# Residual updates of a streaming encoder step: the product with the reciprocal norm formed on GpSimd

## What is computed

```python
def rms_norm(x, g):
    y = x * lax.rsqrt(jnp.mean(x * x, axis=-1, keepdims=True) + EPS)
    return y * g

x = x + rms_norm(mixed,             P['g_post_mix'][l])
x = x + rms_norm(memory_attend(...), P['g_post_mem'][l])
x = x + rms_norm(h @ P['w_down'][l], P['g_post_ff'][l])
```

## Time and profile before

| | us |
|---|---|
| median of 3 runs | 2842.84 |
| the three runs | 2836.05, 2842.84, 2852.88 |
| span of the profiled execution | 2829.8 |
| PE busy | 2645.4 (93%) |
| DVE busy | 1442.4 (51%) |
| ACT busy | 800.5 (28%) |
| POOL busy | 826.6 (29%), 331 low parts |

### The profile page before, as it was taken

The page is one execution under the profiler, slowest core; times in us unless marked ns, Lnnn a source line. Parts: engine busy times, 40 slices in busy tenths (PEclk is TensorE's granted clock), DMA queues, the critical chain, the costliest instruction groups (busy, mean ns, idle before and its releaser), DMA issues.

```text
span 2829.8 us, 47053 instructions
## 1 busy us (share of the span) xinstructions
PE 2645.4 (93%) x18040; PEld 2417.1 (85%) x18040; DVE 1442.4 (51%) x2236; ACT 800.5 (28%) x1460; POOL 826.6 (29%) x335
## 2 busy tenths in 40 slices
PE   8999999999989899999889999999999898999996
PEld 7679888877988799999777798888779787999995
DVE  4661364354464754245656614633554647453366
ACT  4342112234324311111223421122343243111112
POOL 3113222311333143344321132232113232344342
PEclk9999998999999999999999999989999999999998
DMA  4102112222222122222221121122222231222222
GB/s 142 38 23 86 60 47 77 76 75 70 83 71 90 41 83 83 84 83 84 68 77 31 31 90 56 47 84 72 73 71 81 64 94 53 83 84 88 82 83 85
DMA packets 65655, 204.87 MB, mean 72 GB/s; under 512 B 7920, under 2 KB 15984, under 8 KB 65328
## 3 DMA queue, kind: packets, MB, share of 16 engines
q10 hardware_dynamic: 47808, 174.08, 20.2%
q1 hardware_dynamic: 17648, 28.04, 3.0%
HBM read 191.07 MB, written 11.03 MB: 71 GB/s over the span
## 4 chain that ended last, share of the span: by engine, by line
PE 82%; DVE 9%; DVEq 5%; issue 2%; ACT 1%; DMA 0%; SPq 0%; ACTq 0%
PE job L356 65%; PE outp L410 4%; PE scores L385 4%; DVE rstd L1012 3%; PE turn L399 2%; PE job L365 2%; DVEq L1039 2%; PE scores L286 1%; PE scores L388 1%; DVE arena L1003 1%; DVEq L1075 1%; DVE rstd L1020 1%; DVEq L991 1%; DVE x L1040 1%; DVEq L1018 0%
## 5 line engine op out<-in xcount | busy, mean ns | idle before, releaser
L356 PE MATMUL job<-arena,w_hi 128*128 128x288 f32 (+1 forms) x9984 | 1774.2, 299 | 29.9 <-DVE arena L977 8.5
L356 PEld LDWEIGHTS job<-arena,w_hi 128*128 128x128 f32 x9984 | 1491.0, 191 | 52.5 <-issue 20.7
L629 POOL TENSOR_TENSOR w_lo<-raw,w_hi 128x1024 fp32r<-128x1024 f32 x331 | 826.4, 2497 | 1972.3 <-ACT w_hi L648 1972.3
L356 PE MATMUL job<-arena,w_lo 128*128 128x288 f32 (+2 forms) x4992 | 1085.5, 297 | 0.0
L356 PEld LDWEIGHTS job<-arena,w_lo 128*128 128x128 f32 (+1 forms) x4992 | 815.3, 190 | 0.0
L648 ACT ACTIVATE w_hi<-raw 128x1024 fp32r<-128x1024 f32 x331 | 349.7, 1057 | 1086.5 <-PE job L356 899.7
L986 DVE TENSOR_TENSOR tmp<-job,rstd 128x576 f32<-128x576 f32 x70 | 53.0, 758 | 328.1 <-PE job L356 323.6
L410 PEld LDWEIGHTS outp<-probT,v 128*64 128x64 f32 (+2 forms) x992 | 107.5, 145 | 95.7 <-ACT probT L741 46.2
L410 PE MATMUL outp<-probT,v 128*64 128x128 f32 (+2 forms) x992 | 155.4, 284 | 27.5 <-DVE arena L1083 18.4
L286 PE MATMUL scores<-q,const 128*128 128x288 f32 (+1 forms) x296 | 100.0, 476 | 68.2 <-ACT q L709 58.7
L385 PE MATMUL scores<-k,q 128*128 128x256 f32 (+10 forms) x400 | 151.0, 461 | 12.7 <-DVE k L1379 4.4
(11 more groups left out here) (150 smaller groups left out, 1794.1 us busy)
## 6 DMA issues: line engine op xcount, KB each, us to landing
raw<-in_w ACTq DMA_DIRECT2D x332, 512.0 KB, 3.6
bias<-in_bias SPq DMA_DIRECT2D x16, 256.0 KB, 3.4
x<-in_x SPq DMA_DIRECT2D x4, 576.0 KB, 9.1
cs<-in_rope SPq DMA_DIRECT2D x4, 576.0 KB, 4.5
out_o_bandk<-k SPq DMA_DIRECT2D x8, 288.0 KB, 4.3
out_o_bandv<-tmp SPq DMA_DIRECT2D x8, 288.0 KB, 4.6
out_y<-x SPq DMA_DIRECT2D x1, 2304.0 KB, 6.9
bias<-in_mem SPq DMA_DIRECT2D x8, 256.0 KB, 3.6
```

The costliest lines, as they stand in the source:

```text
L356: mm = pe.matmul(ps[0:m, po:po + nn], w[:, s, c:c + m], x[:, k, so:so + nn], start=(k == 0 and w is WHI and x is hl[0]), stop=(k == kt - 1 ...
L629: nc.gpsimd.tensor_tensor(WLO[:, u % RING, :], RAWS[:, u % RAW, :], WHI[:, u % RING, :].bitcast(F32), ALU.subtract).then_inc(lo_done, 1)
```

## The change

In `update_x` DVE no longer forms the scaled sum. After the reciprocal it raises `inverse`. POOL waits for that and forms `UPD[k % 2]` = M[k] x rstd for each of the eight tiles, raising `normed`; from the third tile on it waits until DVE has used the buffer (`act_asked`, two tiles back). DVE waits for `normed` and does X[k] = UPD x gain + X[k] in one instruction, without a drain. To place the products in POOL's order, its loop now runs over layers, with the 164 units of one written out, and the products of an update stand behind the low part of unit `placed + LEAD - 2`, two units past the last one that ACT has placed by then. 24 products per layer, 48 in all.

```diff
+U_MIXED = U_MLA_IN + MLA_HEADS + 3 * U_BRANCH + U_RET + U_BAND + KT
+UPDATES = U_MIXED + 2, U_MIXED + U_MEM + KT // 2, UNITS
...
-            with pool.Fori(0, DEPTH * UNITS, RING) as g:
-                for j in range(RING):
-                    lo(g + j, j)
-            for j in range(LEAD - 1):
-                lo(DEPTH * UNITS + j, j)
+            for u in range(LEAD - 1):
+                lo(u, u)
+            with pool.Fori(0, DEPTH) as l:
+
+                def scale_update(site):
+
+                    pool.wait_ge(inverse, l * len(UPDATES) + site + 1)
+                    for k in range(KT):
+                        if k >= 2:
+
+                            pool.wait_ge(act_asked, l * REQS + AHEAD["ask"] + RET_ASKS + site * KT + k - 1)
+                        nc.gpsimd.tensor_tensor(UPD[:, k % 2], M[:, k], rstd[:, :], ALU.mult).then_inc(normed, 1)
+
+                for u in range(LEAD - 1, UNITS + LEAD - 1):
+                    lo(l * UNITS + u, u)
+                    for site, placed in enumerate(UPDATES):
+                        if u == placed + LEAD - 2:
+                            scale_update(site)
...
-                    def normed(k):
-                        v.scalar_tensor_tensor(out=UPD[:, k % 2], in0=M[:, k], scalar=g_col(name, k),
-                                               in1=rstd[:, :], op0=ALU.mult, op1=ALU.mult)
-
...
                     invert(rstd[:, :])
-                    normed(0)
+                    dve.sem_inc(inverse, 1)
                     for k in range(KT):
-                        dve.drain()
-                        ask(v.tensor_tensor(X[:, k], X[:, k], UPD[:, k % 2], ALU.add))
-                        if k + 1 < KT:
-                            normed(k + 1)
+                        n["normed"] += 1
+                        dve.wait_ge(normed, l * len(UPDATES) * KT + n["normed"])
+                        ask(v.scalar_tensor_tensor(out=X[:, k], in0=UPD[:, k % 2], scalar=g_col(name, k), in1=X[:, k],
+                                                   op0=ALU.mult, op1=ALU.add))
                         if k:
                             low(k - 1)
                     low(KT - 1)
```

More of the change, by code:

```diff
@@ L137 @@
 GATES = 3 * KT + RET_HEADS
-REQS = 3 * KT + RET_HEADS + RET_HEADS // 2
+RET_ASKS = RET_HEADS + RET_HEADS // 2
+REQS = 3 * KT + RET_ASKS
 READY = 42
@@ L266, in build @@
         phase_done = sem("phase_done")
+        inverse, normed = sem("inverse"), sem("normed")
         settled = [sem(f"settled_{e}") for e in ("pe", "dve")]
@@ L948, in _ @@
             with dve.Fori(0, DEPTH) as l:
-                n = counts("job", "gate", "ready", "ask", "done", "item", "store", "rounded")
+                n = counts("job", "gate", "ready", "ask", "done", "item", "store", "rounded", "normed")
                 at = dict(job=0)
@@ L1543, in counted @@
     want = dict(job=JOBS, unit=UNITS, gate=GATES, ready=READY, ask=REQS, item=ITEMS, done=ROOTS,
-                store=STORES, sq=SQUARES, rounded=ROUNDS)
+                store=STORES, sq=SQUARES, rounded=ROUNDS, normed=3 * KT)
     assert all(want[k] + AHEAD.get(k, 0) == v for k, v in n.items()), n
```

## The result

The changed kernel takes 2863.06 us (median of 4 runs, 2860.58 to 2869.91) against 2844.77 us (4 runs, 2836.05 to 2852.88): ratio 1.0074, 95% interval 1.0048 to 1.0099. In a second comparison on one chip it was 2863.23 against 2847.79 us, ratio 1.0060 (1.0041 to 1.0079). It is slower by 15 to 18 us.

What follows compares the result with a forecast made beforehand. DVE was taken to set the pace in the updates, 2.31 us a tile. First and second updates +15.6, third +10.4, together +26.0: 2829.8 + 26.0 + 13.0 = 2868.8, say 2869 us; range 2852 to 2888.

Steps and rivals of the forecast that it cites:

- Direction and cause: In the updates, GpSimd's products and DVE's two-input instructions take turns, so their times add up: 0.9% slower.
- part 2: GpSimd's 128x576 product in the updates: 1.35 us, with a saving possible down to about 1.25.
- part 3: Reciprocal's end to last addition: 8 products, 8 additions, 6 low parts in turns, 21.0 us against 17.16; +3.9 per update.
- Tail: Rounding, square, four matmuls and root behind an update's last addition: claimed unchanged.
- Third update: Weight's low part stands ahead of the first product; last addition +4.7 us, update +5.2, twice: +10.4.
- half charge for slow squares: Third update: paired additions make the second wait about 0.9 us for PE at 1.2 GHz; half taken.
- The base of the sum: Whole kernel: the median lies 13.0 us above the profiled span of 2829.8, taken as what surrounds a span.
- Waits and queues, loop: Engine queues at the updates and GpSimd's written-out loop: nobody waits for the low parts behind; the loop costs nothing.
- Without exclusion: Rival: engines don't exclude each other; pace 1.77 us, -3.1 us four times, third updates about nothing; 2830 us, chance 0.06.
- rival of cheap products and hidden turns: Updates: products of 0.86 to 1.15 us, or DVE start-up partly hidden under turns; within 0.5%, say 2850; chance 0.13.
- The clock rival: PE stays at 1.2 GHz to the end of first and second updates: 2879 us, or 2890 if longer; chance 0.15.
- The signs named beforehand: Updates: DVE instructions of 1.9 to 3.4 us, none inside a product; period near 2.7; reciprocals about 4 further apart; POOL +65.

Runs made afterwards that it cites:

- no_read: Changed kernel, but GpSimd fills each product buffer with a constant instead of M x rstd, a 128x1 product ahead of each fill: 2841.91 us (one run).
- before_again: Unchanged copy of the kernel before, profiled once more: span 2846.1 us, six updates together 153.29 us.
- after_again: Unchanged copy of the changed kernel, profiled once more: span 2856.2 us, six updates together 170.09 us.
- four_buffers: Changed kernel with four product buffers instead of two, so GpSimd may run four tiles ahead: 2863.42 us (10 runs), ratio 1.0066.

## Why the prediction held, point by point

**Direction and cause.** Right. The rows of before already had one addition at 2.74 us and one low part of GpSimd at 3.65, and the same two-way standing still fills the changed update. Products nobody waits for cost 1.16 us each, more buffers gave nothing, half the products cost half of the loss, and a fill that doesn't read cost DVE nothing. The Trainium skill, "SBUF — State Buffer", section "Who interferes with whom", says that a VectorE instruction with two SBUF inputs contends with a GpSimd instruction that reads SBUF, not with one that only writes; the first half agrees with the 1.97 us additions, the second with the 0.81 us ones beside fills in no_read.

**Price of a product (part 2).** Taken as 1.35 alone: 1.38 measured (2.75 for two). The estimate of 1.40 by the Trainium skill, "GPSIMD Engine Reference", section "Elementwise — side-by-side cycle accounting", was as near, on the other side. In its turn it counts 1.28 only: GpSimd's instruction is issued (849.32) before DVE's ends (849.97), and part of its start seems to be over by then; the prediction named this saving (1.25) and didn't take it.

**Sum to the last addition (part 3).** 21.0 us forecast, 19.94 measured. This is the term that was mis-sized: a turn is 1.28 + 0.61 + 0.73 = 2.62 us (2.63 from row to row) instead of 1.35 + 1.44 = 2.79. On both engines an instruction that waits ends sooner behind the other than it would take alone (1.28 for 1.38, 0.61 for 0.73), and DVE's 0.62 behind GpSimd stood in rows 6. Per tile the change takes away 0.67 for the scaled sum and 0.18 of drain, 0.85 in all, and puts in 1.28 + 0.61 - 0.73 = 1.16. The difference of 0.31 over seven tiles is 2.2 us. The first addition starts 1.55 us behind the reciprocal's end instead of 0.99, behind a product instead of a scaled sum, which makes the 2.78 of 19.94 - 17.16; 0.11 of the tail brings it to the 2.89 measured (forecast: 3.9).

**Tail.** Called unchanged. Right in the first update, where the root came 3.04 us behind the last addition before (858.36 - 855.32) and 3.15 after (864.37 - 861.22), the 0.11 above.

**Third update.** 5.2 forecast, 2.6 to 3.6 measured over the pairs of runs. The last addition came 3.67 us later against 4.7 forecast, for the same reason as above. The half charge for slow squares had the wrong sign. It rested on additions that come in pairs 1.4 us apart; but with two buffers GpSimd starts a product only behind the addition two tiles back, the additions ended 2.6 us apart, and only the last two came as a pair (1430.06 and 1431.52). The tail from the last addition to the reciprocal was 4.53 and 3.48 us in the two layers of before, 4.13 and 4.53 in before_again, but 3.49 and 3.48 in after, 3.47 and 3.79 in after_again: in three of the four third updates of before the last squares fell into a spell at the lower level, in the changed kernel the spell was over, or nearly, by then. What ends it isn't shown.

**The sum.** It is 4 x 2.9 + 2.6 + 3.6 = 17.8 us in place of 26.0, so the difference was forecast 8.2 us too large. The forecast time of 2869 still lay only 6 us above the median of 2863.06. That is luck in part: the median of before rose from 2842.84 to 2844.77 with a fourth run, and both medians scatter by a few us.

**The base of the sum.** The 13.0 us between the span of the first profile and the median were taken for what surrounds a span. Wrong: the profiled run of the changed kernel took 2860.58 us with a span of 2858.7, so 1.9 surround it. The rest is about what the short MLP of that one execution (399.5 us, where 409 to 411 is usual) is worth. It didn't hurt, because the difference was set on the median.

**Waits and queues, loop.** As said: GpSimd's next low part came 7.00 us after its last product, and the written-out loop cost nothing.

**The rivals.** Without exclusion the first and second updates would have gained 0.9 us (no_read), not 3.1. The rival's pace of 1.77 took no account of PE's first tiles at 1.2 GHz (3.53 and 2.63 us there), which leave it behind for good. And the third updates, where it put about nothing, came about 5 us shorter in no_read; all six together were 138.7 us against 153, so 14 us less where it named 12, by other parts. (A fill of 0.57 us is shorter than a product, so this is a bound rather than the price of the exclusion.) Of the rival of cheap products and hidden turns the second half came true in part: a turn was 0.16 us shorter than forecast, but the products weren't cheap. The clock rival didn't come about: PE's pause ahead of the update grew from 7.72 to 9.45 us, and it was still back at the 2.4 GHz level by the second tile of the first update (squares of 1.13 us at 849.67) and by the third tile of the other three first and second updates, and stayed there. In the third updates the level did fall again midway (squares of 1.24 us at 1423.68, of 2.15 at 1426.28), in the thin work that the rival named, but it was back for the last squares. The signs named beforehand were seen: additions of 1.9 to 2.0 us, none of them done inside a product, a pace of 2.63. The two reciprocals of a first or second update are 2.9 further apart where "about 4" stood, and POOL's busy time grew by 85, where 65 stood, because an instruction that stands still counts as busy.

## To carry to other kernels

Before work is handed from DVE to GpSimd, ask what both read. If the product and what DVE runs meanwhile each take two tensors from SBUF, the two times add up: here GpSimd's 1.16 us in its turn replaced 0.85 us of DVE. The trace of before answers it, without an experiment, in the longest instances of two-input instructions (2.74 us where the median is 0.76) and what runs beside them. And look at the next bound: even without exclusion the first and second updates gained only 0.9 us each (no_read). A semaphore in place of a drain, which hands nothing over, got 1.0 in a few lines. All six updates then gain 6 to 7 us, 0.2 to 0.3% of the kernel, the edge of what its medians show.

## What was not expected of the hardware

GpSimd waited through a run of four two-input instructions of DVE in rows 7, but the rule isn't plain. In four_buffers, with both engines always ready, POOL's pairs of products took 3.8 us instead of 2.75, as if one DVE instruction had been let in for 1.05, and DVE's merged pair (3.81 us) had a product let in. Which engine gets the next turn wasn't tried by itself.

The MLP of a layer, with the same 2976 matmuls and a granted clock of 1.00, takes 409 to 411 us in 22 of the 24 cases in the twelve profiles, but 399.5 and 401.2 in two. The chain of the first profile of before has one of each kind:

```profile
995.27 397.08 PE job L356 x2976
...
2401.47 387.16 PE job L356 x2976
```

That is 133 against 130 ns a matmul all through the stage. The stretch from the first layer's last reciprocal to the second layer's first update varies too, from 814 to 824 us. The two are of the size of the 10 to 20 us by which runs of one kernel scatter here, and that scatter can hide 4 us of the updates in a median of twelve runs. The cause stays open.
